# Last attention: weighted probabilities turned and moved past stationary values, both key groups in the column halves, all three branches summed in one turned output

## The reference, cut to what matters

```python
s = jnp.einsum('bqghd,bgqkd->bghqk', qr, ks) * scale      # selected blocks: at 512 positions all of them
p = masked_softmax(s, (kpos <= t[:, None])[:, :, None])
o_slc = jnp.einsum('bghqk,bgqkd->bqghd', p.astype(vs.dtype), vs)
...
o_win = jnp.einsum('bghqk,bkgd->bqghd', p.astype(vw.dtype), vw)   # window of 512: the same mask here
return g[..., 0:1] * o_cmp + g[..., 1:2] * o_slc + g[..., 2:3] * o_win
...
attn = attn * jax.nn.silu(z_a)
mix = jnp.concatenate([attn, ssm], axis=-1) @ w_out
```

## Time and profile before

| | us |
|---|---|
| median of 3 runs | 1852.87 (1850.45 to 1854.12) |
| profiled execution, its own time | 1851.63 |
| its span | 1849.5 |
| PE busy | 1762.0 (95%) |
| DVE busy | 1164.7 (63%) |
| ACT busy | 669.3 (36%) |
| chain of waits: PE / DVE / ACT | 80% / 12% / 3% of the span |
| granted TensorE clock, whole span | 0.99 |

### The profile page before, as it was taken

The page is one execution under the profiler, slowest core; times in us unless marked ns, Lnnn a source line. Parts: engine busy times, 40 slices in busy tenths (PEclk is TensorE's granted clock), DMA queues, the critical chain, the costliest instruction groups (busy, mean ns, idle before and its releaser), DMA issues.

```text
span 1849.5 us, 24233 instructions
## 1 busy us (share of the span) xinstructions
PE 1762.0 (95%) x9361; PEld 1465.6 (79%) x9361; DVE 1164.7 (63%) x2372; ACT 669.3 (36%) x1081; POOL 101.9 (6%) x194
## 2 busy tenths in 40 slices
PE   3999989999999999999999999999999999899999
PEld 2777659888888888878888889888888977677787
DVE  6876684876467655655454448875587479545574
ACT  3323573523242334232131325322323332366432
POOL 0001110001000100100000000010001100000000
PEclk9999999999999999999999999999999999999999
DMA  9354331335333525552424223445345322300351
GB/s 366 115 181 161 125 104 69 143 132 169 141 114 114 185 100 174 195 181 85 144 71 147 79 103 125 156 141 187 127 144 182 118 91 91 134 27 20 138 197 46
DMA packets 45470, 245.98 MB, mean 133 GB/s; under 512 B 6256, under 2 KB 6480, under 8 KB 27440
## 3 DMA queue, kind: packets, MB, share of 16 engines
q1 hardware_dynamic: 24848, 155.36, 23.3%
q0 software_dynamic: 20512, 89.11, 14.3%
HBM read 229.23 MB, written 15.22 MB: 132 GB/s over the span
## 4 chain that ended last, share of the span: by engine, by line
PE 80%; DVE 12%; ACT 3%; issue 2%; DMA 2%; SPq 0%; DVEq 0%; ACTq 0%
PE ps L472 69%; DVE w_lo L1474 2%; PE ps L929 2%; DVE ada_raw L1498 1%; PE ps L803 1%; PE ps L910 1%; DMA ada_raw<-in_ada 1%; ACT w_hi L1044 1%; PE ps L919 1%; DVE ada_first L1856 1%; PE ps L651 1%; PE ps L665 1%; PE ps L642 1%; DVE a_p L1958 1%; PE ps L951 1%
## 5 line engine op out<-in xcount | busy, mean ns | idle before, releaser
L1474 DVE TENSOR_TENSOR w_lo<-w_raw,w_hi 128x2048 fp32r<-128x2048 f32 x136 | 311.6, 2291 | 153.7 <-ACT w_hi L1044 153.4
L1044 ACT ACTIVATE w_hi<-w_raw 128x2048 fp32r<-128x2048 f32 x136 | 260.1, 1912 | 361.2 <-PE ps L472 338.4
L472 PE MATMUL ps<-h_hi,w_hi 128*128 128x512 f32 (+1 forms) x1008 | 377.8, 375 | 5.8 <-DVE w_lo L1474 2.4
L472 PE MATMUL ps<-h_lo,w_hi 128*128 128x512 f32 (+1 forms) x1008 | 373.4, 370 | 0.0
L472 PE MATMUL ps<-h_hi,w_lo 128*128 128x512 f32 (+1 forms) x1008 | 373.2, 370 | 0.0
L472 PEld LDWEIGHTS ps<-h_hi,w_hi 128*128 128x128 f32 x1008 | 191.5, 190 | 39.1 <-issue 5.0
L472 PEld LDWEIGHTS ps<-h_hi,w_lo 128*128 128x128 f32 x1008 | 191.2, 190 | 32.3
L472 PEld LDWEIGHTS ps<-h_lo,w_hi 128*128 128x128 f32 x1008 | 191.5, 190 | 30.5
L472 PE MATMUL ps<-hid_hi,w_hi 128*128 128x512 f32 (+1 forms) x576 | 211.3, 367 | 0.0
L472 PE MATMUL ps<-hid_lo,w_hi 128*128 128x512 f32 (+1 forms) x576 | 210.5, 366 | 0.0
L472 PE MATMUL ps<-hid_hi,w_lo 128*128 128x512 f32 (+1 forms) x576 | 210.5, 366 | 0.0
(11 more groups left out here) (395 smaller groups left out, 2476.4 us busy)
## 6 DMA issues: line engine op xcount, KB each, us to landing
w_raw<-in_slabs SPq DMA_DIRECT2D x136, 1024.0 KB, 4.8
ada_raw<-in_ada POOLq DMA_DIRECT2D x104, 512.0 KB, 4.7
s_tables<-s_tab POOLq DMA_DIRECT2D x4, 2692.0 KB, 9.2
s_t<-s_tables POOLq DMA_DIRECT2D x4, 2692.0 KB, 9.8
ada_first<-in_ada SPq DMA_DIRECT2D x16, 512.0 KB, 15.2
a_bias<-in_a_bias POOLq DMA_DIRECT2D x16, 256.0 KB, 3.5
xT<-in_xT SPq DMA_DIRECT2D x4, 512.0 KB, 6.2
s_toeplitz<-KTp POOLq DMA_DIRECT2D x32, 64.0 KB, 3.3
```

The lines of the kernel that those rows point to most:

```text
L472: last = mm(o, l, r, start=start and n == 0, stop=stop and n == 2)
L1044: A(w_hi[s][:], w_raw[:, s, :], ACT.Copy).then_inc(sem("hi_done"), 1)
L1474: tt(w_lo[s][:], w_raw[:, s, :], w_hi[s][:].bitcast(F32), ALU.subtract).then_inc(sem("lo_done"), 1)
```

## The change

The probabilities of a unit are multiplied by 1/sum x gate of their branch before they are turned: two small instructions for a pair of units and one `tensor_scalar` for each unit, on DVE, between ACT's exponent and PE's transposes. The values become the stationary operand (64 columns), the turned probabilities move (128 columns), group 0 into partitions 0 to 63 and group 1 into 64 to 127 of one bank (5 or 6 by turns) per head pair. Both branches and all query tiles of the head pair gather there, and so does the compressed branch, whose probabilities are weighted before their transposes too (`c_scaled`) and whose output is four products into the same bank (`compressed_out`). So a head pair's output stands turned in PSUM, complete; `h_o`, `h_q4` and `c_t`, their instructions, and the 16 transposes behind the loop are gone. `h_gate`, `o_hi` and `o_lo` of a head pair are made in the loop (`OUT_STEPS`). Transposes come at u + 4, products at u + 6 for a pair of units; `h_p` has 6 buffers, `h_pt` 4. Behind the loop `attention_part(0)` stands before `outputs(0)`, and the parts follow as 1; 2, 3; 4, 5; 6. The load of the mixer's second table waits for `c_out` in place of `h_added`.

```diff
-        h_p = at("h_p", 48 * K, [P, 5, T])
-        h_pt = at("h_pt", 58 * K, [P, 3, T])
-        h_o = at("h_o", 72 * K, [P, TT, 512])
+        h_p = at("h_p", 48 * K, [P, 6, T])
+        h_pt = at("h_pt", 60 * K, [P, 4, T])
+        h_gate = at("h_gate", 68 * K, [P, 2, T])
+        o_hi = at("o_hi", 72 * K, [P, 4, T], F32R)
+        o_lo = at("o_lo", 0, [P, 4, T], F32R)
...
-        c_pt = at("c_pt", 91 * K, [P, 2, P])
-        vblk = at("vblk", 92 * K, [P, 4, HD])
+        vblk = at("vblk", 92 * K, [P, 2, H_GROUPS * HD])
...
-        CMP_STEPS = {step: (n // 3, n % 3) for n, step in enumerate((6, 9, 13, 23, 27, 31, 35, 38, 41, 46, 50, 57))}
-        CMP_ADD = {16 * i + 22: i for i in range(4)}
+        CMP_STEPS = {step: (n // 2, n % 2) for n, step in enumerate((6, 13, 23, 31, 35, 41, 46, 52))}
+        CMP_SCALE = {step + 4: i for step, (i, part) in CMP_STEPS.items() if part == 0}
+        OUT_STEPS = {16 * i + 20: i for i in range(4)}
+        ATT_PARTS = (1,), (2, 3), (4, 5), (6,)
...
-                    gp.wait_ge(sem("h_added"), 4)
+                    gp.wait_ge(sem("c_out"), 4)
...
-                elif part == 1:
-                    pe.wait_ge(sem("c_exp"), i + 1)
+                else:
+                    pe.wait_ge(sem("c_scaled"), i + 1)
                     for h in range(2):
                         last = nc.tensor.transpose(ps[7][:, h * P:(h + 1) * P], c_s[:, h * P:(h + 1) * P], ident[:])
                     last.then_inc(sem("c_turned"), 1)
-                else:
-                    for h in range(2):
-                        last = mm(ps[7][:, 256 * h:256 * h + 256], c_pt[:, h, :], vblk[:], start=True, stop=True)
-                    last.then_inc(sem("c_out"), 1)
-
-            for s in range(NUH + 4):
+
+            def compressed_out(i):
+
+                pe.wait_ge(sem("side_free"), C_COPIED[i])
+                for it in range(TT):
+                    last = mm(ps[5 + i % 2][:, it * P:(it + 1) * P], vblk[:, it % 2, :], c_pt[i % 2][:, it // 2, :],
+                              start=False, stop=True, skip_group_check=True)
+                last.then_inc(sem("c_out"), 1)
+
...
-                u = s - 3
+                u = s - 4
...
-                        last = nc.tensor.transpose(ps[3 + u % 2][:, j:j + P], h_p[:, u % 5, j:j + P], ident[:])
+                        last = nc.tensor.transpose(ps[3 + u % 2][:, j:j + P], h_p[:, u % 6, j:j + P], ident[:])
                     last.then_inc(sem("ht_full"), 1)
-                u = s - 4
-                if 0 <= u < NUH:
-                    i, it, br, g = UNITS_H[u]
-                    pe.wait_ge(sem("hpt_ready"), u + 1)
-                    if u % 4 == 0 and u >= 8:
-                        pe.wait_ge(sem("ho_done"), u // 4 - 1)
-                    o, vc = ps[5 + u // 4 % 2][:, (u % 4) * HD:(u % 4 + 1) * HD], slice((br - 1) * P + g * HD, (br - 1) * P + (g + 1) * HD)
+                u = s - 6
+                if u >= 0 and s % 2 == 0:
+                    i, it, br, _ = UNITS_H[u]
+                    pe.wait_ge(sem("hpt_ready"), u + 2)
+                    if u % 16 == 0 and i >= 2:
+                        pe.wait_ge(sem("hxo_gated"), i - 1)
                     for j in range(it + 1):
-                        last = mm(o, h_pt[:, u % 3, j * P:(j + 1) * P], hv[:, j, vc], start=j == 0, stop=j == it)
+                        for g in range(H_GROUPS):
+                            vc = slice((br - 1) * P + g * HD, (br - 1) * P + (g + 1) * HD)
+                            last = mm(ps[5 + i % 2][HD * g:HD * g + HD, it * P:(it + 1) * P], hv[:, j, vc],
+                                      h_pt[:, (u + g) % 4, j * P:(j + 1) * P], start=it == 0 and br == 1 and j == 0, stop=False, skip_group_check=True)
                     last.then_inc(sem("ho_full"), 1)
+                if s in OUT_STEPS:
+                    compressed_out(OUT_STEPS[s])
...
                 for k in range(4):
+                    if o == 0:
+                        pe.wait_ge(sem("hx_done"), k + 1)
                     last = product(b, o % 4, k, o_hi, o_lo)
...
             states(0)
-            pe.wait_ge(sem("h_added"), 4)
-            for i in range(4):
-                transposes([h_o[:, t, i * P:(i + 1) * P] for t in range(TT)], "hxo_full")
+            attention_part(0)
+            c.add("bank", 4)
             for blk in range(NBLK):
                 outputs(blk)
                 if blk + 1 < NBLK:
                     states(blk + 1)
-                    if blk == 0:
-                        pe.wait_ge(sem("hx_done"), 4)
-                    attention_part(2 * blk)
-                    attention_part(2 * blk + 1)
-                else:
-                    attention_part(2 * blk)
+                for o in ATT_PARTS[blk]:
+                    attention_part(o)
                 turn_y(blk)
...
-                u = s - 3
+                u = s - 4
                 if 0 <= u < NUH:
                     n = P * (UNITS_H[u][1] + 1)
                     act.wait_ge(sem("ht_full"), u + 1)
-                    if u >= 3:
-                        act.wait_ge(sem("ho_full"), u - 2)
-                    A(h_pt[:, u % 3, 0:n], ps[3 + u % 2][:, 0:n], ACT.Copy).then_inc(sem("hpt_ready"), 1)
+                    if u >= 4:
+                        act.wait_ge(sem("ho_full"), u // 2 - 1)
+                    A(h_pt[:, u % 4, 0:n], ps[3 + u % 2][:, 0:n], ACT.Copy).then_inc(sem("hpt_ready"), 1)
                 if s < NUH:
                     n = P * (UNITS_H[s][1] + 1)
                     act.wait_ge(sem("hs_done"), s + 1)
-                    if s % 4 == 0 and s >= 8:
-                        act.wait_ge(sem("hw_done"), s // 4 - 1)
-                    A(h_p[:, s % 5, 0:n], h_p[:, s % 5, 0:n], ACT.Exp, bias=neg_max[:, s % 8:s % 8 + 1], scale=-1.0,
-                      accum_out=row_sum[:, s % 8:s % 8 + 1]).then_inc(sem("hp_ready"), 1)
...
+                    if s >= 8:
+                        act.wait_ge(sem("hp_ready"), s - 7)
+                    A(h_p[:, s % 6, 0:n], h_p[:, s % 6, 0:n], ACT.Exp, bias=neg_max[:, s % 8:s % 8 + 1], scale=-1.0,
+                      accum_out=row_sum[:, s % 8:s % 8 + 1]).then_inc(sem("he_done"), 1)
+                if s - 3 in OUT_STEPS:
+                    i = OUT_STEPS[s - 3]
+                    act.wait_ge(sem("hxo_gated"), i + 1)
+                    A(o_hi[:, i, :], h_gate[:, i % 2, :], ACT.Copy).then_inc(sem("hxo_hi"), 1)
...
-            for s in range(NUH + 7):
+            for s in range(NUH + 9):
                 if s < NUH:
                     it = UNITS_H[s][1]
                     n = P * (it + 1)
                     dve.wait_ge(sem("hs_full"), s // 2 + 1)
-                    if s >= 5:
-                        dve.wait_ge(sem("ht_full"), s - 4)
-                    V.tensor_tensor_reduce(out=h_p[:, s % 5, 0:n], in0=ps[s % 3][:, 0:n], in1=h_mask[:, P * (TT - 1 - it):T], scale=-1.0,
+                    if s >= 6:
+                        dve.wait_ge(sem("ht_full"), s - 5)
+                    V.tensor_tensor_reduce(out=h_p[:, s % 6, 0:n], in0=ps[s % 3][:, 0:n], in1=h_mask[:, P * (TT - 1 - it):T], scale=-1.0,
...
-                    elif part == 1:
+                    else:
                         dve.wait_ge(sem("c_exp"), i + 1)
                         step(V.tensor_reduce(cm, cs, AX.X, ALU.add))
                         step(V.reciprocal(cw, cm))
                         step(tt(c_w[:], c_w[:], h_flag[:].unsqueeze(2).to_broadcast([P, TT, H_GROUPS]), ALU.mult))
                         step(tt(c_w[:], c_w[:], h_gts[:, :, 6 * i:6 * i + 6].rearrange("p t (g b) -> p t g b", b=N_BR)[:, :, :, 0], ALU.mult))
-                    else:
-                        dve.wait_ge(sem("c_out"), i + 1)
-                        if i:
-                            dve.wait_ge(sem("h_added"), i)
-                        step(tt(c_t[:], ps[7][:].rearrange("p (j d) -> p j d", d=HD),
-                                cw.unsqueeze(2).to_broadcast([P, TT * H_GROUPS, HD]), ALU.mult))
-                        V.engine_nop().then_inc(sem("side_free"), 1)
-                q = (s - 6) // 4
-                if s >= 6 and s % 4 == 2 and q < NUH // 4:
-                    i, it = UNITS_H[4 * q][0:2]
-                    dve.wait_ge(sem("hp_ready"), 4 * q + 4)
-                    h4 = slice(4 * (q % 2), 4 * (q % 2) + 4)
-                    step(V.reciprocal(row_inv[:, h4], row_sum[:, h4]))
-                    tt(h_w[:, q % 2, :, :], row_inv[:, h4].rearrange("p (b g) -> p b g", g=H_GROUPS),
-                       h_gts[:, it, 6 * i:6 * i + 6].rearrange("p (g b) -> p b g", b=N_BR)[:, 1:N_BR, :], ALU.mult).then_inc(sem("hw_done"), 1)
-                q = (s - 8) // 4
-                if s >= 8 and s % 4 == 0 and q < NUH // 4:
-                    i, it = UNITS_H[4 * q][0:2]
-                    dve.wait_ge(sem("hw_done"), q + 1)
-                    dve.wait_ge(sem("ho_full"), 4 * q + 4)
```

(55 more changed lines are left out.)

34 lines of the change are left out of this document (12 added, 22 removed).

## The result

The changed kernel takes 1857.14 us (median of 14 runs, 1853.99 to 1861.81) beside 1853.38 for the kernel before (14 runs): ratio 1.0023, 95% interval 1.0016 to 1.003. It is slower by 4 us. The forecast was 1845.1, range 1837 to 1855, and gave slower 0.13: wrong in sign, and outside the range.

A forecast was written before the change was run, and what follows sets the result against it. PE was taken to bound the last attention's loop (busy 131.8 of 138.3 us). From 1851.63, less 5.1 in the loop and 2.7 behind it, gave 1843.8, plus 1.2 for the median: 1845.1 us; range 1837 to 1855.

The forecast's parts named there:

- Products -12.6: PE in the loop: products with the values fall from 35.2 to 22.6 us, as column halves run side by side.
- transposes +5.8: PE in the loop: each of 64 groups of four transposes takes 0.59 us in place of 0.50.
- Idle 8.2: PE's idle time in the loop, taken midway between 6.5 and 9.8 us.
- 125.0 busy: PE's busy time in the loop falls from 131.8 to 125.0 us; with idle the loop takes 133.2.
- Rival B: Loop: PE's idle rises to the first attention's 13.1 us, loop 138.1, total 1850.0; chance 0.22.
- Rival C: Loop: PE's transposes wait for DVE's scaling in each pair, 0.7 us, 18.2 in all; total 1861.6; chance 0.11.
- A: Loop: transposes stay as cheap as before, so it gains 12.6 us; total 1837.5; chance 0.15.
- D: Loop: product halves do not overlap, 0.112 us a record, +6.4 on PE; total about 1857; chance 0.02.
- Behind the loop -2.7: From loop end E to the second `outputs`: E + 22.0 in place of E + 24.7, gain 2.7 us.
- DVE under 90 us: DVE's busy time in the loop, forecast at 82.7 us; over 90 was named as a sign of being wrong.
- signs named for being wrong: Profile after: long L2230 waits, transposes 0.50, 16 product records 1.8, `states(1)` waiting for a table, DVE over 90 us.
- waits for L2230: Loop: PE's transposes (L923) waiting for DVE's scaling; more than 10 us in total would point to idle or scaling rivals.

The follow-up runs named there:

- The old order: Changed kernel with the attention projection's first part put back behind the next block's states, as in the kernel before: 1863.06 us (10 runs).
- the waits filled: Changed kernel with 13 unused matmuls on PE at five places where it waits before the clock falls: 1856.87 us (12 runs).
- two fillers: Changed kernel with scaling first, silu moved, more lag, earlier first split, and four unused matmuls, two ahead of the first z tile: 1840.94 us, ratio 0.9936.

## Why the prediction was wrong

- **Products -12.6, transposes +5.8 on PE: right.** The prices hold (1.02, 0.59). At full clock PE's busy time fell by 7.4 to 9.0, beside 6.8 forecast.
- **Idle 8.2: wrong**, measured 13.8, 5.6 us more. The upper end, the 13.1 of the first attention, was nearest; I took off its 3.3 us of start and then halved the way to today's idle. This loop has a start of its own (0.9 and 0.8 us), a silu in front of copies (2.1), and compressed work of 1.3 to 1.5 us on DVE ahead of scalings (1.8 and 1.5).
- **The term that was missing: the clock.** The step "125.0 busy" took rows at full clock and let nothing follow from idle time. It cost 8.6 us in the loop by half of the low time (about 5 by the fit), more than the whole 6.8 that PE was to save. It stood in the profile: the earlier trace rows give 0.96 for the first attention, the stretch from which I took form and idle, and 0.98 for the loop itself. Of its 115.6 us, 0.04 is some 9 us of low time.
- **Rival B** (idle as in the first attention, loop 138.1) had the mechanism and nearly the idle. With the clock's 8.6 it gives 146.7, against 145.6. **Rival C** put the price at waits in each pair; there were 7 waits, of 5.6 us together, not 18. (By its own sum with 26 pairs it comes out slower from 0.5 us for a pair on, not 0.4.) **A** and **D** fell by the prices of the groups.
- **Behind the loop -2.7: right**, -2.5. The first `outputs` came at E + 8.4, the second at E + 22.2, with 22.0 forecast. The old order costs 4.2 us in its profile and not 2.7: its longer wait was followed by 6.8 us at half clock, for which the sum had no term either.
- **DVE under 90 us: right** (80.0), and no comfort. The 14.5 us more of it delayed PE at the start, though DVE idled 65 us of the loop. None of the signs named for being wrong came (the waits for L2230 are 5.6 us, under the 10): the list, too, had nothing on the clock.
- **Chances.** Slower had 0.13, nearly all of it in C (0.10) and D (0.02). A term that can only cost, and that grows with every wait, belonged to the forecast, B and C alike; with 8 us on B's 1850 the range would have reached 1858.

The Trainium skill, "TensorE: Matmul & The Clock Gate", in A second HAM failure mode: psum-queue depth-cycling, tells of a kernel in which short idle times between groups of matmuls make the clock swing. The runs here agree: 23.9 us of low time behind waits of 0.8 to 2.1 us, and 3.3 with the waits filled.

## What to carry to other kernels

Where a change makes the engine that bounds a stage cheaper but lengthens the chain in front of it, price each new wait on TensorE with what its clock may lose behind it, here 3.4 to 13.7 us at half speed for single waits of 1.5 to 2.1 us, or two or three of 0.2 to 0.9 close together. Read the granted clock of each stretch before a price is carried over from it. Then order the in-order engines so that the short work that TensorE waits for comes first, and put the long pieces (a silu with its table loads, a split) where TensorE has a long tile to do.

## What the hardware did that was not expected

- A wait of 2.06 us cost about as much afterwards as by itself: taking it away gave 5.4 us of the median, and by the fit 2.1 of the gain came by the clock.
- Half of the profiles (7 of 14 kernels, that with two fillers ahead of it not among them) begin the loop at half clock, 3.2 to 3.4 us of low time from its first tile on. PE idles 0.8 and 1.0 us shortly before it in these seven, but in the other six without a filler there too, so these waits alone do not decide it. What the seven have in common lies earlier: they show 6.8 us of low time between 1570 and 1583, in code that is the same in all 14, where the others show 3.4. How the one brings the other is not shown.
- Unused work can be worth its time: two kernels that differ by three matmuls of 512 columns differ by 10.3 us of low time in the loop (13.7 and 3.4) and 3.9 us of median; their mean clocks, 0.9854 (10 runs) and 0.9890 (6 runs), differ by 13 us of low time.
- The same wait at the same place brings a fall in one kernel and none in another: 2.93 us behind the loop, 1.83 and 1.47 us in it. Nothing here shows what decides it.
